# Recurrent stage: decay sums of four levels per matmul, and weight splits moved to the stage's end

## The reference, cut to what matters

```python
def step(s, xs):
    qc, kc, vc, gc = xs                       # gc: log of the forget gate
    a = jnp.cumsum(gc, axis=2)
    inter = jnp.einsum('bhtk,bhkv->bhtv', qc * jnp.exp(a), s)
    diff = a[:, :, :, None, :] - a[:, :, None, :, :]
    decay = jnp.exp(jnp.where(tri[:, :, None], diff, -jnp.inf))
    scores = jnp.einsum('bhtk,bhsk,bhtsk->bhts', qc, kc, decay)
    intra = jnp.einsum('bhts,bhsv->bhtv', scores, vc)
```

## Time and profile before

| | us |
|---|---|
| median of 3 runs | 2930.79 (2928.8 to 2932.57) |
| the profiled execution, its own time | 2930.48 |
| its span in the trace | 2928.7 |
| recurrent stage in it, first sums to end of the last `out_pair` | 1885.75 to 1990.33 |
| `out_pair` begins, four pairs | 1912.00, 1936.98, 1961.94, 1984.81 |

### The profile page before, as it was taken

How to read it: one execution, slowest core, us unless ns; L and a number is a source line. 1 busy time by engine, 2 the same in 40 slices (tenths; PEclk the granted TensorE clock), 3 DMA queues, 4 the chain that set the end, 5 groups by cost and what they waited for, 6 DMA issues and landing times.

```text
span 2928.7 us, 35096 instructions
## 1 busy us (share of the span) xinstructions
PE 2843.4 (97%) x13294; PEld 2363.7 (81%) x13294; DVE 2008.1 (69%) x2284; ACT 1359.9 (46%) x1673; POOL 140.5 (5%) x102
## 2 busy tenths in 40 slices
PE   8998999999999999999999999999989999999998
PEld 6886788888888887787788888888868888888886
DVE  4665879798798887776685487575655467745455
ACT  4446454443443454555444444654444444344443
POOL 0000010010010100000000000000001001010010
PEclk9999999999999999999999999999989999999999
DMA  6861889987878987655666666404645588755654
GB/s 209 239 193 63 280 266 311 315 267 276 282 263 299 315 286 268 181 184 181 199 186 198 194 186 184 132 1 141 212 151 168 191 264 275 256 179 186 192 187 144
DMA packets 323470, 622.55 MB, mean 213 GB/s; under 512 B 27447, under 2 KB 29623, under 8 KB 321975
## 3 DMA queue, kind: packets, MB, share of 16 engines
q1 hardware_dynamic: 320471, 602.02, 63.8%
q10 hardware_dynamic: 2848, 18.49, 1.7%
HBM read 614.14 MB, written 7.24 MB: 212 GB/s over the span
## 4 chain that ended last, share of the span: by engine, by line
PE 84%; DVE 6%; issue 5%; DMA 2%; ACT 2%; POOL 0%; POOLq 0%; SPq 0%; DVEq 0%; ACTq 0%
PE ps L1290 78%; DVE wlo L1767 2%; DVE macc L1946 1%; DMA raw<-w_in 1%; PE ps L1270 1%; PE ps L1443 1%; PE ps L1401 1%; ACT whi L665 1%; PE ps L1643 1%; PE ps L1661 1%; PE ps L1623 1%; DVE tcol L2068 0%; DMA raw<-w_o 0%; PE ps L1372 0%; DMA raw<-w_up 0%
## 5 line engine op out<-in xcount | busy, mean ns | idle before, releaser
L1767 DVE TENSOR_TENSOR wlo<-raw,whi 128x1024 fp32r<-128x1024 f32 x940 | 1165.9, 1245 | 788.2 <-ACT whi L665 783.7
L665 ACT ACTIVATE whi<-raw 128x1024 fp32r<-128x1024 f32 x940 | 995.8, 1060 | 1308.5 <-PE ps L1290 1184.7
L1290 PE MATMUL ps<-whi,hhi 128*128 128x512 f32 x2064 | 811.2, 393 | 2.5 <-DVE hlo L2074 2.3
L1290 PE MATMUL ps<-whi,hlo 128*128 128x512 f32 x2064 | 804.1, 390 | 0.0
L1290 PE MATMUL ps<-wlo,hhi 128*128 128x512 f32 x2064 | 803.8, 389 | 0.0
L1290 PE MATMUL ps<-whi,xhi 128*128 128x512 f32 x1632 | 646.0, 396 | 16.1 <-DVE wlo L1767 13.4
L1290 PE MATMUL ps<-wlo,xhi 128*128 128x512 f32 x1632 | 638.3, 391 | 0.0
L1290 PE MATMUL ps<-whi,xlo 128*128 128x512 f32 x1632 | 638.1, 391 | 0.0
L1290 PEld LDWEIGHTS ps<-whi,hhi 128*128 128x128 f32 x2064 | 388.0, 188 | 83.5 <-DVE hlo L2074 3.4
L1290 PEld LDWEIGHTS ps<-whi,hlo 128*128 128x128 f32 x2064 | 387.7, 188 | 81.7
L1290 PEld LDWEIGHTS ps<-wlo,hhi 128*128 128x128 f32 x2064 | 388.1, 188 | 79.7 <-issue 1.0
(11 more groups left out here) (272 smaller groups left out, 1554.7 us busy)
## 6 DMA issues: line engine op xcount, KB each, us to landing
raw<-w_in SPq DMA_DIRECT2D x296, 512.0 KB, 4.3
raw<-mlp_w SPq DMA_DIRECT2D x256, 512.0 KB, 3.8
mraw<-w_mod SPq DMA_DIRECT2D x192, 512.0 KB, 6.2
raw<-w_up SPq DMA_DIRECT2D x128, 512.0 KB, 4.9
raw<-w_down SPq DMA_DIRECT2D x128, 512.0 KB, 5.4
raw<-w_o SPq DMA_DIRECT2D x32, 512.0 KB, 5.3
raw<-w_ple_gate SPq DMA_DIRECT2D x32, 512.0 KB, 4.0
raw<-w_out SPq DMA_DIRECT2D x32, 512.0 KB, 3.8
```

What stands on the lines that cost most here:

```text
L665: nc.scalar.activation(whi[:, s % NSLOT], raw[:, s % NSLOT], ACT.Copy).then_inc(hi_done, 1)
L1290: ins = nc.tensor.matmul(ps[:, bank(par) + th], a[:, kt, th * P:(th + 1) * P], b[:, (s + u) % NSLOT, k], start=(kt == 0 and m == 0), stop= ...
L1767: nc.vector.tensor_tensor(wlo[:, s % NSLOT], raw[:, s % NSLOT], whi[:, s % NSLOT].bitcast(F32), ALU.subtract)\
```

## The change

The exponents of four levels are now formed together. A level step belongs to a group `g` of four levels, a head `h` and a token half `th`, and runs 4 matmuls of 512 columns (two directions, high and low part). There are still 8 level steps per pair and 1024 columns per exponential. `dec` has two parts of 16 KB, the whole of `whi` and of `wlo`, one for each group. A group's first level now waits for four exponentials. Group 0 holds the levels of 64, 32, 16 and 8 tokens, group 1 those of 4, 2 and 1 and the cross step; its steps with `th == 0` need two ACTIVATEs, of 6 and 2 planes, since the cross planes lie at different ends. No weight piece of `pw` can be split before the stage, so all three are split at its end (`held=3`).

```diff
-        dec = [at("dec%d" % n, [P, 2, 4, 2 * TH, P // 2], F32, a + 8 * K) for n, a in enumerate((whi_at, wlo_at))]
+        dec = [at("dec%d" % n, [P, 4, 4, 2 * TH, P // 2], F32, a) for n, a in enumerate((whi_at, wlo_at))]
-        ESTEPS = [("level", u, h) for u in range(4) for h in range(2)] + [("init", 0, 0)]
+        ESTEPS = [("level", g, h, th) for g in range(2) for h in range(2) for th in range(TH)] + [("init", 0, 0, 0)]
...
             def exp_step(pair, k):
-                    if pair == 0 and u < 2:
-                        act.wait_ge(pe_done, plan["pw"][0])
-                    elif h == 0:
-                        before = (pair, u - 2) if u >= 2 else (pair - 1, u + 2)
-                        act.wait_ge(qk_done, before[0] * N_S + 2 * before[1] + 3)
+                    if k % 4 == 0:
+                        if pair == 0:
+                            act.wait_ge(pe_done, plan["pw"][0])
+                        else:
+                            act.wait_ge(qk_done, (pair - 1) * N_S + 5 if g == 0 else pair * N_S)
+                    dst = dec[g][:].rearrange("p l (s d) k c -> p d (l s) k c", d=2)[:, :, :, 2 * h + th]
+                    if g and th == 0:
+                        nc.scalar.activation(dst[:, :, 0:6], src[:, :, 2:8], ACT.Exp)
+                        nc.scalar.activation(dst[:, :, 6:8], src[:, :, 0:2], ACT.Exp).then_inc(d_done, 1)
...
             for pair in range(NPAIR):
...
                 exp_step(pair, 5)
                 if more:
                     turned_rows(pair + 1, 2)
+                exp_step(pair, 6)
+                if more:
                     forget_high(pair + 1)
                 if pair:
                     out_scaled(pair - 1)
-                exp_step(pair, 6)
                 exp_step(pair, 7)
...
-                    act.wait_ge(qk_done, pair * N_S + 7)
-                    split(pw0 + 2, 2)
+                    act.wait_ge(qk_done, pair * N_S + 5)
+                    for n in range(3):
+                        split(pw0 + n, n)
                 far_queries(pair)
                 if more:
                     exp_step(pair + 1, 2)
+                    exp_step(pair + 1, 3)
                 out_squares(pair)
-                if more:
-                    exp_step(pair + 1, 3)
...
             def sums_step(pair, k):
...
-                    for th in range(TH):
-                        out_of = ps[:, b + th].rearrange("p (l r c) -> p l r c", l=2, r=4)
-                        for d in range(2):
-                            m = sums_of(u, d, th)
-                            for n, w in enumerate(parts(h, d, th)):
-                                ins = nc.tensor.matmul(out_of[:, :, 0:4:3] if d == 0 else out_of[:, :, 1:3], w,
-                                                       sums_r[:, m:m + 2].rearrange("p l (r c) -> p l r c", r=2), start=n == 0, stop=n == 1)
+                    for d in range(2):
+                        m = sums_of(g, d, t_)
+                        for n, w in enumerate(parts(h, d, t_)):
+                            ins = nc.tensor.matmul(ps[:, b + d], w, sums_r[:, m:m + 4].rearrange("p l c -> p (l c)"),
+                                                   start=n == 0, stop=n == 1)
...
             def decay_step(pair, j):
...
-                dve.wait_ge(d_done, pair * N_E + 2 * u + 2)
+                dve.wait_ge(d_done, pair * N_E + 4 * g + 4)
...
-            split(pw0 + 2, 2)
+            for n in range(3):
+                split(pw0 + n, n)
```

More of the change, by code:

```diff
@@ L57 @@
 LEVELS = [64, 32, 16, 8, 4, 2, 1]
-N_SUMS = 2 * (len(LEVELS) - 1) + 8
+N_SUMS = 18
 NHEAD = B_H + A_Q
@@ L96, in shape_constants @@
         bwd = np.where(second, (j >= mid) & (j < q), (j >= q) & (j < mid))
-        split.append((fwd[:, np.concatenate([first, first + m])], bwd[:, np.concatenate([first + m, first])]))
+        split.append((fwd[:, np.concatenate([first, first + m])], bwd[:, np.concatenate([first, first + m])]))
     pre_in, suf_ex, suf_in, pre_ex = (np.broadcast_to(x, (P, P)) for x in (j <= q, j > q, j >= q, j < q))
     sums = []
-    for a in range(0, len(LEVELS) - 1, 2):
-        for d in range(2):
-            sums += [split[a][d], split[a + 1][d]]
+    for d in range(2):
+        sums += [split[a][d] for a in range(4)]
     for d, cross in enumerate(((suf_ex, pre_in), (suf_in, pre_ex))):
-        for th in range(TH):
-            sums += [split[-1][d], cross[th]]
+        sums += [cross[0]] + [split[a][d] for a in range(4, len(LEVELS))] + [cross[1]]
     s, tt = j, q
@@ L1120, in _ @@
                     chunk(pn + 8 * c, evac_to(row, c * NCH, gn + c, ACT.Sigmoid), extra=slots(early_slots, 32 * n + 8 * c),
-                          held=1 if n and c == 3 else 0)
+                          held=3 if n and c == 3 else 0)
             def exp_step(pair, k):
-                kind, u, h = ESTEPS[k]
+                kind, g, h, th = ESTEPS[k]
                 e = pair * N_E + k
@@ L1668, in _ @@
                 score_step(pair, 0)
+                sums_step(pair, 4)
                 if more:
@@ L1671, in _ @@
                 score_step(pair, 1)
-                sums_step(pair, 4)
+                sums_step(pair, 5)
                 if more:
@@ L1675, in _ @@
                 score_step(pair, 2)
-                sums_step(pair, 5)
+                sums_step(pair, 6)
                 if more:
@@ L1679, in _ @@
                 score_step(pair, 3)
-                sums_step(pair, 6)
+                sums_step(pair, 7)
                 score_step(pair, 4)
-                sums_step(pair, 7)
-                score_step(pair, 5)
                 sums_step(pair, 8)
-                score_step(pair, 6)
-                if more:
-                    sums_step(pair + 1, 0)
-                score_step(pair, 7)
-                if more:
-                    sums_step(pair + 1, 1)
-                score_step(pair, 8)
-                if more:
-                    sums_step(pair + 1, 2)
+                for n in range(4):
+                    score_step(pair, 5 + n)
+                    if more:
+                        sums_step(pair + 1, n)
                 out_pair(pair)
-                if more:
-                    sums_step(pair + 1, 3)
             def o2_turn(g):
@@ L2264, in _ @@
                 for c in range(4):
-                    chunk(pn + 8 * c, extra=slots(early_slots, 32 * n + 8 * c), held=1 if n and c == 3 else 0)
+                    chunk(pn + 8 * c, extra=slots(early_slots, 32 * n + 8 * c), held=3 if n and c == 3 else 0)
             def decay_step(pair, j):
```

37 lines of the change are left out of this document (20 added, 17 removed).

## The result

The changed kernel took 2934.76 us (median of 20 runs, 2931.78 to 2938.99), the kernel before 2931.15 beside it (20 runs, 2928.4 to 2934.04): a ratio of 1.0013 with a 95% interval of 1.0007 to 1.0019. That is 3.6 us more, slower, but within the 0.2% that was set as the bound of a change. The forecast was 2933.2. The profiled execution took 2934.50, its span 2932.7.

A forecast was written before the change was run, and what follows sets the result against it. In the recurrent stage no engine is full; a chain of waits over PE, ACT and DVE bounds it. First pair +1.0, middle pairs +0.8, last +0.6 give +2.4 us: 2932.9 profiled, 2933.2 median, range 2928.5 to 2938.5.

The forecast's parts named there:

- periods of 25.4: Sign of being right: 25.4 us between `out_pair` starts; periods under 24.9 would show it wrong.
- Part 1, the wide matmul: Sums steps on PE: four 512-column matmuls take 0.91 us per step where eight of 256 took 0.95.
- The rival of cheap wide matmuls: Sums steps on PE: four wide matmuls take only 0.48 us, total 2929.1 us; chance 0.1.
- Part 2, the step moved: Sums step 3 leaves its place behind `out_pair` (start O); third turn ends at O + 10.56 us.
- Part 3, the later exponential: Fifth level waits for four exponentials on ACT, starting at O + 15.15 us, not 14.06: front part 1.1 longer.
- Part 4, `far_queries` earlier: Back part of middle pairs: ACT is free sooner, `first_queries` follows the cross copy, 0.69 us shorter.
- Part 5, the first pair: First level waits for four exponentials, its copy ends at 1893.8: start +1.3 us, whole pair +1.0.
- Part 6, the last pair: Last exponential before the fifth level ends at O + 12.5 us: pair 0.6 us longer.
- Part 7, the splits: Weight splits at the stage's end on ACT and DVE are hidden: 0 us, at most 2.4 on the path.
- The clock rival: PE's 2.3 us gap before the sixth score lowers its clock: +1.9 us per middle pair, 2938.0; chance 0.2.
- The fifth level was late: Judges the rival that the fifth level still starts at O + 14.06: total 2930.4 us; chance 0.1.
- The planes cost nothing: Judges the rival that spread decay planes slow DVE products by 0.13 us each: total 2940.5; chance 0.05.

The follow-up runs named there:

- experiment 1: Changed kernel with ACT running the pair's last level exponential ahead of `out_scaled`: 2932.95 us, ratio 1.0005 to the kernel before.
- experiment 2: Kernel before, groups of two levels kept, with only the change's sums-step order on PE and the next pair's fourth exponential ahead of `out_squares`: 2929.43 us, ratio 0.9991.
- experiment 3: Changed kernel with every 512-column sums matmul cut into two of 256 columns: 2935.78 us, ratio 1.0016 to the kernel before.
- experiment 4: Changed kernel with unread matmuls filling PE's waits in all four pairs: 2933.99 us, ratio 1.0009 to the kernel before.
- experiment 9: Changed kernel again with nothing changed, one profiled execution: 2931.94 us.
- experiment 10: Changed kernel again with nothing changed, one more profiled execution: 2932.79 us.
- experiment 5: Kernel before with all three weight splits at the stage's end and the first diagonal behind the last weight chunk: 2929.37 us, ratio 1.0004.
- experiment 6: Kernel before with unread matmuls filled in behind scores of the last pair: 2927.71 us, ratio 0.9998.
- experiment 7: Kernel of experiment 2 with row turns ahead of their sums steps and the second half's logarithms moved later: 2923.53 us, ratio 0.9982 to the kernel before.
- experiment 11: Kernel before again with nothing changed, one profiled execution: 2930.11 us.
- experiment 12: Kernel before again with nothing changed, one more profiled execution: 2927.11 us.
- experiment 8: Kernel of experiment 7 with unread matmuls filled in behind scores of the last pair: 2923.40 us, ratio 0.9985 to the kernel before.

## Why the prediction was right

The direction, the size to 1.6 us and the place (the stage) were right, and the later exponential, its mechanism, is shown by experiments 1 and 2. Not all went as drawn: it named a granted clock under 1 before the last pair as a sign of being wrong, and the profile has one; it named periods of 25.4, and of the two middle pairs only the third has that (25.41, and 26.16 for the second). Of the 3.63 us by which the stage grew, 2.4 were forecast. At full clock it is 3.08, where the first pair has 0.2 more than forecast, the middle pairs 0.1 and the last 0.4. The rest, 0.56, is the net of the falls of the clock in these two executions, where the forecast had none. That both executions have one in the last pair, at nearly the same price, is luck. By the prediction's own steps:

**Part 1, the wide matmul: right.** 0.91 forecast, 0.92 to 0.94 measured, and experiment 3 puts the whole gain at about 0.1 per pair. The rival of cheap wide matmuls is dead: 0.23 per matmul of 512 columns in a stream with weight loads. The figure of the Trainium skill's "TensorE: Matmul & The Clock Gate", section "Back-to-back issue gap", some 131 ns, is not what this kernel's matmuls took.

**Part 2, the step moved: right.** Third turn at O + 10.61 for 10.56.

**Part 3, the later exponential: right.** Fifth level at O + 15.20 for 15.15. The split exponential took 0.95 from its start to that of the next instruction, where 1.01 had been taken. That is below the lower bound of 0.98: half of the 1.96 that two exponentials take up to the end of the second counts that end in. Experiment 1 shows that this ACT queue is the cause, experiment 2 that two exponentials instead of four would have left it off the chain.

**Part 4, `far_queries` earlier: right.** `first_queries` stands behind the cross copy, and the sums step ahead of `out_pair` is covered. At full clock a middle pair is 25.41 to 25.43, for a forecast of 25.4.

**Part 5, the first pair: +1.0 forecast, +1.18 measured.** Level start and copy are as forecast (1894.34, less the 0.48 by which the stage began later, is 1893.86, for 1893.8). The fifth level then starts 1.66 later in the stage than before (1903.00 - 0.48 against 1900.86), and the back part gives 0.47 back.

**Part 6, the last pair: +0.6 forecast, +0.98 measured.** The exponential ended at O + 12.4, for 12.5. But the level did not start then. The chain in the last pair:

```profile
1976.56 1.07 ACT dec L1140
...
1977.65 0.02 DVEq L2277
1977.67 0.40 issue
1978.07 0.10 DVE kD L2295
```

VectorE took 0.40 from seeing the semaphore to its start, where a few hundredths pass in the first and the third pair. Experiments 1, 3, 4, 9 and 10 have the same 0.40 there, so it is no accident of one execution. It is about the size of this term's error (0.38). Its cause is open, and no run was made for it.

**Part 7, the splits: right**, by experiment 5 and by the rows of DVE above.

**The clock rival came true in part.** Falls follow the longer waits (table above), and the comparison with experiment 4 gives the price in the profiled execution: 26.16 - 25.43 = 0.73 in one pair. The forecast of 1.9 was mis-sized. It took the fall's length, 6.9 us, from the last pair; in a middle pair the clock was back after 3.4 us (1930.8 to 1934.2), in every one of the seven falls counted above. The last pair has both: 6.8 us in six profiles, 3.4 in experiment 1. That dense work behind the gap makes it short would fit the middle pairs, but no run tested it. And the rival gave a fall to both middle pairs, where 5 of 8 had it. Nor did a fall that "comes sooner" cost the last pair anything: both kernels have one there in some executions, 2.5 in before's profile (22.87 + 5.52 less 22.03 + 3.84) and 2.4 in after's (23.95 + 5.26 less 23.01 + 3.84). So after - before is 3.08 + 0.73 - 0.17 = 3.64, the 3.63 of the table but for rounding.

The Trainium skill, in "TensorE: Matmul & The Clock Gate", section "What's actually happening", says that the gate looks at PE's activity in windows that run free of the kernel. The runs fit this, without showing the windows: behind the same wait the clock fell in the second pair of one execution and in the third of another. So a single profile can't tell what falls cost on average, and it could not here: experiment 6 removed 2.5 us from a profile and 1.3 from a median.

**The other rivals.** The fifth level was late. The planes cost nothing: a product of the third pair took 0.68 to 0.70, the one-token level's keys 0.82 as before.

What was not seen: that the order alone is a gain, and the group of four its undoing. The prediction summed the parts, +1.1 and -0.7, and did not ask what the -0.7 would be worth with groups of two. Experiments 2 and 4 put a price on the group. With its last `out_pair` at 3.84 experiment 2 would have a stage of 100.23, which makes the group 104.95 - 100.23 = 4.7 us. But the fall in experiment 2 begins ahead of that, and stretches its cross score to 2.08. With the 21.12 that the last pair takes at full clock in experiment 7, with the same order on PE in that pair, the group costs an estimated 5.6 us. It is the net of all that goes with it: the wide matmul's 0.1 per pair, the exponential in two instructions and the open 0.40.

## What to carry to other kernels

When several small steps of a producer are merged, or a consumer waits for a larger group, write down the last member of the group, and all that stands ahead of it on its in-order engine: that moment, not the sum of the work, is the consumer's start. Test the order and the grouping apart, since a gain of one can hide in the loss of the other. When a change lengthens the wait of a busy TensorE, look at the granted clock behind that wait in more than one profile before a fall is charged to the change.

## What the hardware did that was not expected

- A wait of 2.4 us of PE between dense stretches was followed by 3.4 us at 1.2 GHz in 5 of 8 cases, and one of 1.5 us in 2 of 7. With the wait filled by unread matmuls down to 0.5 us there was none in the two middle pairs of one execution.
- The fall in the last pair, which the profile before shows, is not in all executions of the same kernel: 3.84 us for `out_pair` in experiments 11 and 12, 5.52 in the first profile.
- In the last pair, VectorE started 0.40 us after its semaphore was seen, in all six profiles with groups of four. Open.
- In the first pair the products that run beside GpSimd's multiplication (1905.20 to 1907.86, L2471) take longer: 0.68, then 1.53 and 0.99 in the changed kernel; a product of 1.53 stands beside it in the kernel before as well. In experiments 7 and 8, where the logarithm and with it the multiplication come some 9 us later in the stage, all products of this size in the first pair's end took 0.68 to 0.82.

```profile
1905.42 1.53 DVE L2296 TENSOR_TENSOR qD<-qT,dec 128x512 f32<-128x512 f32 x1
...
1907.51 0.99 DVE L2295 TENSOR_TENSOR kD<-kT,dec 128x512 f32<-128x512 f32 x1
```
